# Forget-gate decay as two short-format rows, the last expert's output by halves, and per-token means as TensorE products, in a four-layer fp32 transformer kernel

## The reference, cut to what matters

```python
def moe_swiglu(xn, router, w_gu, w_down):
    ...
    for e in range(N_EXPERTS):
        out = out + comb[..., e:e + 1] * swiglu(xn, w_gu[e], w_down[e])
def first_block(...):
    ...
    h = h + moe_swiglu(rmsnorm(h, od_norm_moe[i]), od_router[i], od_moe_gu[i], od_moe_down[i])
    return rmsnorm(h, final_norm)
def second_block(...):
    for l in range(DEPTH):                       # 2 layers
        xn = _rms_norm(x, attn_norm[l])
        h = xn @ w_in[l]                         # mla, fox q k v, moba, diff, mem columns
        ...
        log_f = jax.nn.log_sigmoid(fox_f.astype(jnp.float32) + fox_b_f[l].astype(jnp.float32))
        decay = jnp.cumsum(log_f, axis=1).transpose(0, 2, 1)
        o_b = _dense_causal_attention(_rms_norm(q_b, fox_q_norm[l]), _rms_norm(k_b, fox_k_norm[l]),
                                      v_b, HEAD_DIM ** -0.5, decay)
# in _dense_causal_attention, for a block of 128 queries:
#   s = q k^T * scale + (decay[query] - decay[key]), masked, softmax, times v
```

## Time and profile before

| | |
|---|---|
| Median of 3 executions | 2436.09 us |
| Lowest and highest of them | 2434.79 and 2438.53 us |
| Profiled execution, own time | 2437.17 us |
| Its span, first to last instruction | 2435.4 us |
| PE busy | 2359.9 us, 97% of the span |
| DVE busy | 1805.1 us, 74% |
| ACT busy | 1369.9 us, 56% |
| POOL busy | 130.4 us, 5% |
| Chain that ended last | PE 81%, DVE 9%, DMA 4%, ACT 4%, POOL 1% |
| Granted PE clock, mean of the span | 0.986 |

### The profile page before, as it was taken

One profiled execution on the slowest core, in us unless ns is written; L12 is line 12 of the kernel. 1 busy time (PEld: TensorE's weight loads), 2 busy tenths in 40 slices (PEclk: granted clock), 3 DMA queues, 4 the chain that ended last, 5 costly groups with the idle time before them and its releaser, 6 DMA issues.

```text
span 2435.4 us, 33655 instructions
## 1 busy us (share of the span) xinstructions
PE 2359.9 (97%) x14448; PEld 2102.1 (86%) x14448; DVE 1805.1 (74%) x1835; ACT 1369.9 (56%) x1347; POOL 130.4 (5%) x107
## 2 busy tenths in 40 slices
PE   5999999999999999999999999998999999999999
PEld 5999999788988888888888888886789999888999
DVE  5666556776688888888888888886667676756766
ACT  4345444464577776776777777775445444544433
POOL 2001000001100000000000000002310001301000
PEclk9999999999999999999999999999999999999999
DMA  5653546354499999999999999994333554323553
GB/s 192 203 181 124 185 150 225 123 194 132 144 369 352 345 346 352 349 349 341 349 348 357 348 351 346 348 374 154 112 112 116 194 193 163 121 96 101 190 178 104
DMA packets 309644, 566.92 MB, mean 233 GB/s; under 512 B 12338, under 2 KB 137553, under 8 KB 309360
## 3 DMA queue, kind: packets, MB, share of 16 engines
q1 hardware_dynamic: 305792, 560.39, 66.2%
q10 hardware_dynamic: 3696, 4.30, 0.5%
HBM read 563.60 MB, written 1.05 MB: 232 GB/s over the span
## 4 chain that ended last, share of the span: by engine, by line
PE 81%; DVE 9%; DMA 4%; ACT 4%; POOL 1%; issue 1%; ACTq 0%; DVEq 0%; SPq 0%; POOLq 0%
PE bank L996 20%; PE bank L787 15%; PE bank L1014 10%; PE bank L637 7%; PE bank L771 7%; PE bank L625 6%; PE bank L250 5%; DVE wL L202 4%; DMA raw<-in_od_moe_gu 3%; ACT wH L231 2%; PE bank L647 2%; PE bank L613 2%; PE bank L1271 2%; PE bank L1323 2%; DVE arena L202 1%; DVE ra L205 1%
## 5 line engine op out<-in xcount | busy, mean ns | idle before, releaser
L202 DVE TENSOR_TENSOR wL<-raw,wH 128x2048 fp32r<-128x2048 f32 (+3 forms) x541 | 1209.6, 2243 | 359.1 <-ACT wH L231 356.4
L231 ACT ACTIVATE wH<-raw 128x2048 fp32r<-128x2048 f32 (+3 forms) x541 | 1014.3, 1877 | 542.6 <-DMA raw<-in_od_moe_gu 104.1
L996 PE MATMUL bank<-wH,ra 128*128 128x512 f32 x1792 | 578.0, 394 | 3.8 <-DVE wL L202 3.4
L996 PEld LDWEIGHTS bank<-wH,ra 128*128 128x128 f32 x1792 | 336.5, 188 | 77.6 <-DVE wL L202 4.5
L787 PE MATMUL bank<-ra,wH 128*128 128x256 f32 x2112 | 383.6, 284 | 5.3 <-DVE ra L205 5.3
L996 PE MATMUL bank<-wL,ra 128*128 128x512 f32 x896 | 349.0, 389 | 0.0
L787 PEld LDWEIGHTS bank<-ra,wH 128*128 128x128 f32 x2112 | 329.5, 192 | 8.1 <-DVE ra L205 6.9
L787 PE MATMUL bank<-ra,wL 128*128 128x256 f32 x1056 | 298.8, 283 | 0.0
L1014 PE MATMUL bank<-wH,ra 128*128 128x512 f32 x896 | 288.3, 393 | 2.6 <-DVE ra L202 2.3
L637 PE MATMUL bank<-wH,ra 128*128 128x512 f32 (+2 forms) x800 | 225.6, 364 | 4.5 <-DVE ra L205 4.5
L1014 PEld LDWEIGHTS bank<-wH,ra 128*128 128x128 f32 x896 | 168.9, 189 | 39.6 <-DVE ra L202 2.5
(11 more groups left out here) (204 smaller groups left out, 2604.1 us busy)
## 6 DMA issues: line engine op xcount, KB each, us to landing
raw<-in_od_moe_gu SPq DMA_DIRECT2D x224, 1024.0 KB, 6.5
raw<-in_od_moe_down SPq DMA_DIRECT2D x112, 1024.0 KB, 6.7
raw<-in_ev_ffn_gu SPq DMA_DIRECT2D x22, 1024.0 KB, 5.2
raw<-in_ffn_w_gate SPq DMA_DIRECT2D x22, 1024.0 KB, 5.4
raw<-in_ffn_w_up SPq DMA_DIRECT2D x22, 1024.0 KB, 5.4
raw<-in_ffn_w_down SPq DMA_DIRECT2D x22, 1024.0 KB, 5.0
raw<-in_xa_wkv SPq DMA_DIRECT2D x16, 1024.0 KB, 5.2
raw<-in_od_pw_w SPq DMA_DIRECT2D x12, 1024.0 KB, 5.2
```

What stands on the lines that cost most here:

```text
L202: self.op.tensor_tensor(out, a, b, op).then_inc(*self.sig.up(name))
L231: self.op.activation(out, a, ACT.Copy, **kw).then_inc(*self.sig.up(name))
L996: m = p.op.matmul(out[:, :], a, b, start=half == 0 and c == 0 and i == 0, stop=half == 1 and c == 3 and i == 2)
```

## The change

It has three parts.

1. In `pe_moe_down`, for the very last round of the last expert only, the products run bank by bank: bank 0 with half 0 and half 1, then bank 1 with both. ACT's copy of bank 0 waits for the new signal `down_first` (the 12th of 24 products) and no longer for the last. The weight block of half 0 is now released with the 18th product, not with the 12th.
2. In layer 0 of the second block both means come from one PE step, `pe_two_means`: 16 fp32 products of a 128x128 chunk of squares with two columns `wm`, right behind the mla columns. POOL's two totals, the separate "s0" mean, ACT's second squaring and the scale `w2` go away. ACT squares two chunks with one instruction (it did one chunk at a time).
3. The decay of the queries is dropped (it is the same for all keys of a row, and the softmax takes it out). That of the keys is stored in fp32r, with 128 rows: row h has head h's high part, row 32 + h its remainder, in both layers. PE makes it with 2 products instead of 4, DVE with one 128x256 and one 32x256 instruction. For each head the scores take one fp32r product over 128 rows: `head_row` (ones in rows h and 32 + h, written once by four DVE additions in `dve_head_rows`) times `decay`.

The diff, cut to its core:

```diff
@@ -1003,17 +1001,20 @@
                 self.wait_bank(p, i, (self.act, self.dve)[i], ("y", e, i))
-        for half in range(2):
+        very_last = h == NE * NRD - 1
+        for half, n in [(x, n) for n in range(2) for x in range(2)] if very_last else [(x, n) for x in range(2) for n in range(2)]:
             tag = ("moe", e, f, "down", half)
             wh, wl = self.pe_block(p, tag, 2)
-            for n in range(2):
-                for c in range(2):
-                    ns = slice(n * 512, (n + 1) * 512)
-                    xh, xl = hv[0][:, 2 * half + c], hv[1][:, 2 * half + c]
-                    for i, (a, b) in enumerate(passes(xh, xl, wh[:, c, ns], wl[:, c, ns])):
-                        m = p.op.matmul(self.banks[n][:, :], a, b, start=f == 0 and half == 0 and c == 0 and i == 0,
-                                        stop=f == NRD - 1 and half == 1 and c == 1 and i == 2, skip_group_check=True)
-            m.then_inc(*self.pe.up(("block", self.index[tag]), *([("down", h)] if half else [])))
+            for c in range(2):
+                ns = slice(n * 512, (n + 1) * 512)
+                xh, xl = hv[0][:, 2 * half + c], hv[1][:, 2 * half + c]
+                for i, (a, b) in enumerate(passes(xh, xl, wh[:, c, ns], wl[:, c, ns])):
+                    m = p.op.matmul(self.banks[n][:, :], a, b, start=f == 0 and half == 0 and c == 0 and i == 0,
+                                    stop=f == NRD - 1 and half == 1 and c == 1 and i == 2, skip_group_check=True)
+            if n:
+                m.then_inc(*self.pe.up(("block", self.index[tag]), *([("down", h)] if half else [])))
+            elif very_last and half:
+                m.then_inc(*self.pe.up("down_first"))
@@ -1121,7 +1122,10 @@
         columns("mla", 1)
-        self.pe_token_mean(p, (s, "w"), self.wsq)
+        if l:
+            self.pe_token_mean(p, (s, "w"), self.wsq)
+        else:
+            self.pe_two_means(p, s)
@@ -1133,8 +1137,6 @@
         self.pe_qk_turn(p, s, l, "fox")
-        if l == 0:
-            self.pe_token_mean(p, "s0", self.sq)
@@ -1210,6 +1212,17 @@
+    def pe_two_means(self, p, s):
+        b = self.bank(p, (s, "w"), self.dve, ("s0", "mean"))
+        p.wait_ge(*self.pool.of("wm"))
+        for c in range(C):
+            p.wait_ge(*self.act.of(((s, "w"), "sq", c // 2)))
+            for t in range(2):
+                m = p.op.matmul(b[:, 2 * t:2 * t + 2], self.wsq[:, c, t * 128:(t + 1) * 128], self.wm[:, c, :],
+                                start=c == 0 and t == 0, stop=c == C - 1, skip_group_check=True)
+        m.then_inc(*self.pe.up((s, "w")))
@@ -1243,9 +1256,7 @@
         p.wait_ge(*self.pool.of((s, "lz")))
-        for c in range(2):
-            m = p.sum(b[0:96, c * 256:c * 256 + 256], [(self.lz[:, j, 32 * c:32 * c + 96], self.tri[:, j, :]) for j in range(2)])
-        m.then_inc(*self.pe.up((s, "decay")))
+        p.sum(b[:, 0:256], [(self.lz[:, j, :], self.tri[:, j, :]) for j in range(2)]).then_inc(*self.pe.up((s, "decay")))
@@ -1702,7 +1713,7 @@
                         a.wait_ge(*self.pe.of(("mix_in", pe_ - 1, 7)))
-                    a.wait_ge(*self.pe.of(("down", q - 1)))
+                    a.wait_ge(*self.pe.of("down_first" if q == NE * NRD else ("down", q - 1)))
@@ -1818,9 +1828,7 @@
             a.cp((s, "x_hi", c), self.X8[0][:, c, :], self.hT[:, c, :], scale=self.gain(l, c))
-            if l == 0:
-                a.do(((s, "w"), "sq", c // 2), self.wsq[:, c, :], self.hT[:, c, :], ACT.Square, scale=self.w2[:, c:c + 1])
-            elif c % 2:
+            if c % 2:
@@ -1860,13 +1868,9 @@
         blocks("in", l, "diff_qk", 1)
-        if l == 0:
-            a.wait_ge(*pe.of("logits"))
-            for j in range(4):
-                a.do(("s0", "sq", j), self.sq[:, 2 * j:2 * j + 2, :], self.hT[:, 2 * j:2 * j + 2, :], ACT.Square)
...
         self.act_squares(a, s, "mem_k", self.sq_mem, self.mkv[:, :, 0:256], (dve, ("mkv", l, 1)), (act, ("mkv", l, 0)),
-                         (self.pool, ((s, "w"), "total")))
+                         (pe, (s, "w")))
@@ -2625,8 +2629,8 @@
                          [[(t[part(64 * (h % 2), 64), h // 2, qs], t[part(64 * (h % 2), 64), 2 + h // 2, 0:nk]),
-                           (self.decay[part(64 * (h % 2), 2), 0, h // 2, qs], self.decay[part(64 * (h % 2), 2), 1, h // 2, 0:nk])]
-                          for h in order], (dve, (s, "decay")))
+                           (self.head_row[:, h, :], self.decay[:, 0:nk])]
+                          for h in order], (dve, (s, "decay")), (dve, "head_row"))
                 elif g == "mla":
@@ -2776,6 +2780,21 @@
+    def dve_head_rows(self, v):
+        for h in range(4):
+            v.tt("head_row", self.head_row[:, h, :], self.ident[:, h:h + 1].broadcast_to([128, 128]),
+                 self.ident[:, 32 + h:33 + h].broadcast_to([128, 128]), ALU.add)
+    def dve_decay(self, v, s):
+        ps = self.ps((s, "decay"))
+        v.wait_ge(*self.pe.of((s, "decay")))
+        v.ts(None, self.decay, ps[:, 0:256], -1.0, ALU.mult)
+        v.own()
+        v.stt((s, "decay"), self.decay[32:64, :], ps[32:64, 0:256], -1.0, self.decay[32:64, :].bitcast(F32), ALU.mult, ALU.subtract)
@@ -2876,7 +2895,15 @@
         self.dve_lambda(v, s, l)
-        self.dve_mean(v, (s, "w"), self.sc, EPS * EPS if l == 0 else EPS)
+        if l == 0:
+            self.dve_head_rows(v)
+        if l:
+            self.dve_mean(v, (s, "w"), self.sc, EPS)
+        else:
+            both = self.ps((s, "w"))[:, 0:4].rearrange("p (t k) -> p t k", t=2)
+            v.wait_ge(*self.pe.of((s, "w")))
+            v.ts(((s, "w"), "mean"), self.sc, both[:, :, 1], EPS * EPS, ALU.add)
+            v.ts(("s0", "mean"), self.inv_tok, both[:, :, 0], EPS, ALU.add)
@@ -2921,17 +2948,10 @@
         columns("fox_v")
-        fx = CS["fox"]
-        v.wait_ge(*self.pe.of((s, "decay")))
-        v.own()
-        for i in range(2):
-            v.ts((s, "decay"), self.decay[0:96, i], self.ps((s, "decay"))[0:96, :].rearrange("p (c t) -> p c t", c=2),
-                 self.cst[0:96, fx + 2 * i:fx + 2 * i + 1], ALU.mult, self.cst[0:96, fx + 2 * i + 1:fx + 2 * i + 2], ALU.add)
+        self.dve_decay(v, s)
...
         blocks("in", l, "diff_v", 0)
-        if l == 0:
-            self.dve_mean(v, "s0", self.inv_tok, EPS)
@@ -3085,16 +3105,12 @@
-        f, w, k = self.cols[:, COL["final_norm"]:COL["final_norm"] + 8], self.small[:, 342:350], self.w2
+        f, w = self.cols[:, COL["final_norm"]:COL["final_norm"] + 8], self.small[:, 342:350]
         g.wait_ge(*self.got["cols"].of("cols"))
-        g.wait_ge(*self.dve.of("eps"))
         g.tt(None, w, f, f, ALU.mult)
+        g.fill(None, self.wm[:, :, 0], 1.0 / D)
         g.own()
-        g.ts(None, w, w, EPS, ALU.add)
-        g.own()
-        g.tt(None, k, w, self.epst[:, 1:2].broadcast_to([128, 8]), ALU.pow)
-        g.own()
-        g.tt("w2", k, k, w, ALU.mult)
+        g.ts("wm", self.wm[:, :, 1], w, EPS, ALU.add, 1.0 / D, ALU.mult)
@@ -3126,7 +3142,8 @@
         g.wait_ge(*self.dve.of((s, "x_lo", 7)))
-        self.pool_total(g, (s, "w"), self.wsq)
+        if l:
+            self.pool_total(g, (s, "w"), self.wsq)
@@ -3148,16 +3165,13 @@
         for x in range(2):
-            for c in range(2):
-                g.ts((s, "lz"), self.lz[:, :, 32 * c + x:128:64], xf[:, :, 2 * c:2 * c + 2], 8.0, ALU.mult)
+            g.ts((s, "lz"), self.lz[:, :, 32 * x:32 * x + 4], xf, 8.0, ALU.mult)
...
         if l == 0:
-            self.pool_total(g, "s0")
+            self.pool_power(g, "s0", self.inv_tok, ("s0", "mean"))
...
         self.pool_power(g, (s, "diff"), sums["diff"], (s, "ms", "diff"))
-        if l == 0:
-            self.pool_power(g, "s0", self.inv_tok, ("s0", "mean"))
```

13 lines of the change are left out of this document (6 added, 7 removed).

## The result

The changed kernel takes 2418.83 us (median of 4 executions, 2417.95 to 2422.18), the kernel before 2437.02 in the same comparison (4 executions). The ratio is 0.9931 with a 95% interval of 0.9915 to 0.9947: 18.2 us less by the medians, where 15.1 less were forecast. The profiled execution of after has a span of 2417.6 us, 17.8 less than that of before. Lines of the code are two lower than before in the helpers (L637 is now L635, L647 is L645, L202 is L200), and L1271 is L1282.

What follows compares the result with a forecast made beforehand. PE was busy 2359.9 of 2435.4 us, so gains had to come from its work, waits or clock. From 2436.09, +0.1 - 1.7 - 0.9 - 4.8 - 7.8 = -15.1 gave 2421.0 us, range 2416.5 to 2430.5.

Steps and rivals of the forecast that it cites:

- Part 1: Last expert's end: ACT's earlier copy of bank 0 gains nothing behind the later weight conversion; +0.1 us, bounds -0.7 and +1.3.
- bank 1 is needed only for the second half of the spreading: Last expert: DVE's copy of bank 1, about 1.4 us later, still comes just in time for PE's spreading products.
- Part 2: Layer 0's means: cost 1.9, PE's wait before mla turns -3.56, turns at full clock -1.6, new slow stretch +1.6; together -1.7 us.
- The stretch at 1.2 GHz that I booked behind the small products: Behind the new two-column mean products in layer 0: a low-clock stretch, a little likelier than not, booked at +1.6 us.
- Part 3a: Making the decay: DVE's two instructions take 1.0 instead of 1.53 us, about -0.45 a layer; -0.9 us, bounds 0 and -1.6.
- Part 3b: Fox scores, both layers: one fp32r decay pass and less standstill at the mask save 4.8 us, bounds -5.6 and 0.
- My terms for the decay product: Fox scores: each decay product saves 0.165 us with 128 keys, 0.326 with 256; four of either length a layer.
- My term for the mask's standstill: Fox scores: the mask, now following a 128-row product, loses some 0.15 us of standstill in each of 4 banks a layer.
- The banks that I named as a sign: Fox scores: banks of about 1.2 us with 128 keys and 1.9 with 256 would show the forecast right.
- Part 3c: Clock in the fox pieces: three stretches at 1.2 GHz vanish, worth -7.8 us, bounds -7.8 and 0; the largest single guess.
- clock 1.00 in all four fox pieces: Sign of being right: full granted clock in both fox pieces of both layers; near 0.5 there would show it wrong.
- Rival B: Fox scores: the low clock stays or moves as narrow products remain; only -7.3 us, 2428.8, chance 0.20.

Runs made afterwards that it cites:

- e2: The kernel before with only both means as small TensorE products in layer 0: 2429.59 us, ratio 0.9983.
- e4: The changed kernel with ACT's second squaring and POOL's s0 total back in layer 0, the total unused: 2420.05 us, ratio 0.9944.
- e3: The changed kernel with the last expert's down products in the old order: 2415.76 us, ratio 0.9922.
- e7: The changed kernel with ACT's and DVE's copies of the last expert's banks ahead of the mla weights' conversion and remainder: 2416.58 us, ratio 0.9923.
- e10: The changed kernel with fox scores grouped over both banks and the last expert's copies ahead of the mla weights' conversion and remainder: 2407.39 us, ratio 0.9899.
- e8: The changed kernel with the 16 decay products read as plain fp32, same 128 rows, two passes each: 2417.34 us, ratio 0.9934.
- e1: The kernel before with only the decay change (fp32r, 128 rows, both layers): 2420.93 us, ratio 0.9950.
- e11: The kernel before with its 64-row and 2-row fp32 fox score products grouped within each bank: 2427.76 us, ratio 0.9980.
- e6: The changed kernel with the even heads' decay products over 64 rows, the odd heads' still over 128: 2410.39 us, ratio 0.9912.
- e5: The changed kernel with each bank's fox scores grouped, both heads' q times k, then both decay products, then mask: 2408.72 us, ratio 0.9896.
- e9: The changed kernel with fox scores grouped over both banks, four q times k, then each bank's decay products and mask: 2407.70 us, ratio 0.9903.

## Why the prediction was right, and where it was not

The mechanism was right in the large, and each term can be held against the pieces.

**Part 1, forecast +0.1, measured +0.4.** The step "bank 1 is needed only for the second half of the spreading ... I take that as just in time" failed. The products were in time; the flag's branch behind them in PE's queue was not. I had looked for who waits for DVE's copy among products only. The bounds, -0.7 and +1.3, hold it.

**Part 2, forecast -1.7, measured -3.5.** The cost was 1.6 instead of 1.9 (32 passes in 3.48 us, 0.109 each), the wait -3.5, and the turns at full clock -1.6, shown by e2 and e4. The stretch at 1.2 GHz that I booked behind the small products did not come in the profiled execution. Of the ten kernels that have these products it came in four (e3, e4, e7, e10; 7.2 us behind the means instead of 5.6), and this trace did without: that the term was saved is luck of the execution.

**Part 3a, forecast -0.9, measured -0.2.** The reading was right, the size was not. DVE is the later one in both layers, so PE's four passes bring nothing by themselves, and DVE's path became 0.86 us shorter and not 0.45: 0.70 from the two instructions and the rest from the gap ahead of them. Layer 0 shows it beside e2, where the decay is the old one and everything else stands as in the changed kernel:

```profile
1723.16 0.71 PE L1283 MATMUL bank<-arena 96*128 96x128 f32 x4 [1.72 <-DVE arena L211]
```

This product comes 8.01 us behind the turns of mla in e2 and 7.15 in the changed kernel, and the piece is 18.64 against 17.77 us. So each layer gives 0.87 at full clock. In layer 1 a stretch at 1.2 GHz that begins right behind the wait (granted 1.2 GHz from 2102.3 on) took 1.5 us back. I had no term for it.

**Part 3b, forecast -4.8.** At full clock the four pieces are 2 x 10.67 + 2 x 12.08 = 45.5 us; before, at full clock, they are 58.4 less the 7.8 that I had worked out, so 50.6. That is -5.1. My terms for the decay product, 0.165 and 0.326 us each, make 3.9 for both layers, and e8 shows 3.6 for the format. My term for the mask's standstill, 0.15 in each bank, makes 1.2; from before to e8 a bank gains 0.18 (1.97 to 1.79 and 2.81 to 2.63), 1.4 in all. That is one change of rows fewer, since the mask now follows a product of 128 rows. So both terms were right. The banks that I named as a sign, 1.2 us with 128 keys and 1.9 with 256, don't follow from these terms: 1.97 less 0.48 is 1.49, and 2.81 less 0.80 is 2.01, and 1.51 and 2.00 were measured.

**Part 3c, forecast -7.8.** 47.1 - 45.5 = 1.6 us is lost in these pieces where it was 7.8, so -6.2. "I expect all three stretches to vanish" came true as worded, and a shorter one came in the first piece of layer 0, which had been clean; so the sign "clock 1.00 in all four fox pieces" failed in one. That the clock would come back was a guess, and why it did is not shown. Rival B is excluded for these pieces by e1. A further 3.1 us came behind the fox scores of layer 1 and 1.4 in layer 0, in pieces that the change doesn't touch. I had no term for them. They go with stretches at 1.2 GHz that moved or went. In both layers of before PE waits 1.43 us for DVE some 23 us behind the fox scores. In the changed kernel a stretch lies ahead of that place, PE comes later, and the wait is gone: a low clock ahead of a wait is in part free. The rest, in layer 1, is about one stretch fewer. By the medians part 3 alone brings 12.5 us, and in its trace the decay and fox pieces hold 12.6 (11.3 and 1.3), so nothing is left for later ones. With all parts, 18.2 us stand against 14.6 in the changed pieces. Whether those 3.6 us follow from the change or from the executions compared isn't settled.

The forecast of 2421 is 2.2 us above the measured 2418.8. In the profiled execution the terms missed by +0.3 (part 1), -1.8 (part 2), +0.7 (3a) and +1.3 (3b and 3c), and -4.5 of later pieces and +1.4 ahead of the last round had no term: together -2.6, which is, but for rounding, the difference between -15.1 and the profile's -17.8. Misses of +3.7 and -6.3 partly cancel, so that the sum came this near is in part luck.

What stays open: what exactly makes the clock fall. It fell behind waits (e4's turns), and less of it fell with fewer standstills (e11, one trace); fewer rows in use did not bring it down (e6).

## What to carry to other kernels

Count changes of the number of rows on TensorE before counting passes: putting products of one kind together was worth another 7 to 9 us here by the ratios (e5, e9, e10). When a copy or a wait moves, look in the waiting engine's queue for what isn't a product, such as a branch. And an idle engine's additions next to VectorE's two-input instructions are not free, even where nobody waits for their result.
